# Six of nine token tiles take their u scores from a dense product; only v rows are gathered for them

## The reference

```python
# per token: 8 heads x top 16 of 128 x 128 = 16384 experts -> 128 experts
expert = take_along_axis(cand_id, top_i)
gate = softmax(top_v)
act = gelu(einsum('thkd,td->thk', u_tab[expert], xb))     # 128 dots of 1024 per token
out = einsum('thk,thkd->td', gate * act, v_tab[expert])   # 128 weighted rows of 1024
```

## Time and profile before

| | us |
|---|---|
| median of 3 runs | 4585.86 |
| lowest and highest | 4565.0, 4586.57 |
| span of the profiled execution, first to last instruction | 4574.9 |

### The profile page before, as it was taken

How to read it: one execution, slowest core, us unless ns; L and a number is a source line. 1 busy time by engine, 2 the same in 40 slices (tenths; PEclk the granted TensorE clock), 3 DMA queues, 4 the chain that set the end, 5 groups by cost and what they waited for, 6 DMA issues and landing times. The chain is left out here.

```text
span 4574.9 us, 46652 instructions
## 1 busy us (share of the span) xinstructions
PE 3277.9 (72%) x15679; PEld 1680.7 (37%) x15679; DVE 2488.2 (54%) x7735; ACT 801.6 (18%) x1284; POOL 1648.0 (36%) x1379
## 2 busy tenths in 40 slices
PE   8899997736389666686678676667666667666666
PEld 2798896636056441341145344124210101111110
DVE  2245553126764445577755454557786555555554
ACT  2232333232014113110013211211000100000000
POOL 1211104523245444442345444344333333333332
PEclk9999998968589886897789888678765666666666
DMA  7211103533789889898889898999899999999998
GB/s 278 73 58 49 39 29 131 171 118 111 274 334 407 338 354 379 345 384 341 337 348 405 345 393 356 383 375 362 354 387 360 415 404 405 409 412 409 414 411 346
DMA packets 243430, 1400.14 MB, mean 306 GB/s; under 512 B 30661, under 2 KB 47685, under 8 KB 100986
## 3 DMA queue, kind: packets, MB, share of 16 engines
q0 software_dynamic: 156672, 1140.92, 62.1%
q1 hardware_dynamic: 86522, 256.22, 15.5%
HBM read 1345.59 MB, written 51.43 MB: 305 GB/s over the span
## 5 line engine op out<-in xcount | busy, mean ns | idle before, releaser
L1057 DVE CUSTOM_DVE_ANT_0 peer_uv<-peer_uv,all_PS 128x512 f32<-128x512 f32 x2176 | 1435.3, 685 | 1164.2 <-DMA peer_uv<-in_uv,peer_idx 804.8
L996 PE MATMUL all_PS<-peer_hT,peer_sel 96*128 96x512 bf16 x2176 | 1002.4, 484 | 1027.4 <-DVE peer_halves L1057 842.5
L979 POOL DMA_INDIRECT peer_uv<-in_uv,peer_idx x1088 | 1043.4, 959 | 1756.9 <-PE all_PS L1015 1379.6
L996 PEld LDWEIGHTS all_PS<-peer_hT,peer_sel 96*128 96x128 bf16 x2176 | 203.0, 102 | 2002.9 <-DVE peer_halves L1057 1632.6
L1015 PE MATMUL all_PS<-peer_uv,peer_zw 128*32 128x512 f32 x4352 | 871.7, 849 | 2.4 <-DVE peer_zw L1077 2.4
L867 POOL TENSOR_TENSOR flow_w_lo<-flow_w,flow_w_hi 128x1024 fp32r<-128x1024 f32 (+1 forms) x204 | 460.4, 2261 | 456.5 <-ACT flow_w_hi L860 455.9
L1031 ACT ACTIVATE peer_ge<-peer_pre 128x4 f32<-128x4 f32 x272 | 55.7, 205 | 2109.7 <-DVE peer_pre L1063 2109.6
L887 PE MATMUL all_PS<-mix_h_hi,flow_w_hi 128*128 128x384 f32 (+1 forms) x672 | 279.6, 416 | 32.2 <-POOL flow_w_lo L867 31.8
L860 ACT ACTIVATE flow_w_hi<-flow_w 128x1024 fp32r<-128x1024 f32 (+1 forms) x204 | 203.5, 1003 | 359.2 <-PE all_PS L889 110.7
L888 PE MATMUL all_PS<-mix_h_lo,flow_w_hi 128*128 128x384 f32 (+1 forms) x672 | 226.3, 337 | 0.0
L889 PE MATMUL all_PS<-mix_h_hi,flow_w_lo 128*128 128x384 f32 (+1 forms) x672 | 226.1, 336 | 0.0
(11 more groups left out here) (290 smaller groups left out, 4670.4 us busy)
## 6 DMA issues: line engine op xcount, KB each, us to landing
cond_w<-in_w_ada SPq DMA_DIRECT2D x12, 2048.0 KB, 8.1
flow_w<-in_w_gate_ab SPq DMA_DIRECT2D x48, 512.0 KB, 7.1
flow_w<-in_w_query SPq DMA_DIRECT2D x48, 512.0 KB, 7.7
flow_w<-in_w_conv SPq DMA_DIRECT2D x36, 512.0 KB, 4.5
peer_uv<-in_uv,peer_idx POOLq DMA_INDIRECT x1088, 10.4
gla_w<-in_w_heads SPq DMA_DIRECT2D x24, 512.0 KB, 4.4
flow_w<-in_w_proj_b SPq DMA_DIRECT2D x24, 512.0 KB, 7.8
flow_w<-in_w_out SPq DMA_DIRECT2D x24, 512.0 KB, 8.4
```

What stands on the lines that cost most here:

```text
L979: self.nc.gpsimd.indirect_dma_start(out=self.uv[:, n % self.NUV, :], out_offset=None, in_=self.A["uv"], in_offset=bass.IndirectOffsetOnAxi ...
L996: nc.tensor.matmul(PS[:, f, :], self.sel[:, c:c + 1].broadcast_to([3 * GR, P]), self.hT[:, g % self.NH, f * 512:(f + 1) * 512], start=True ...
L1057: nc.vector.tensor_tensor_reduce(part, part, PS[:, f, :], 1.0, 0.0, ALU.mult, ALU.add, self.halves[:, d, f, e:e + 1]).then_inc(M["dotted"], 1)
```

## The change

Tiles of blocks 1 and 2 (six of nine, 768 tokens, `SCORED`) no longer gather u rows. Their pick phase also runs the whole product h @ u^T, for its block's three tiles: the transposed u table comes as 128 pieces of 0.5 MB (`u_chunks`) through the same stream, each 512 experts wide and two k-tiles deep; per piece and tile TensorE makes six matmuls of 128x512, 18 per piece, 2304 per block. A chunk of four pieces ends in three PSUM banks, which ScalarE copies and SyncE writes to a scores array in DRAM (25 MB per block). When such a token's turn comes, `fetch` issues two indirect DMAs: 128 v rows of 4 KB, and 128 single values of its scores. There is no spread, dot or join for it; gelu reads the fetched scores. The first 320 tokens go as before.

With it: slots are 18 of 4 KB per partition (a dotted token takes two, nine wide ones in all), GpSimd may fetch up to 12 tokens ahead where slots are known free, but not across the table phase; the stream's raw buffers are 4 for 2; in block 2 the low halves are made by VectorE (`make_low_on_vector`); the bf16 splits of h are made for dotted tiles alone; and each block has shares of its own. They put 148 of block 0's 296 tokens ahead of the table phase and 148 in it, and 153 of block 1's 384 ahead and 231 in it.

```diff
+SCORED = frozenset(range(3, NT))
+CHUNK, KPAIR = 512, 2
+NCHUNK, NKP = NK * NK // CHUNK, KD // KPAIR
...
-    def __init__(self, sc, sources, raws=2, pairs=4):
+    def __init__(self, sc, sources, by_vector, raws=4, pairs=4):
...
+    def make_low_on_vector(self, nc, dve, i):
+        if i < len(self.sources) and i in self.by_vector:
+            nk = self.sources[i].shape[1]
+            if i - 1 not in self.by_vector:
+                dve.wait_ge(self.low, i)
+            dve.wait_ge(self.high, i + 1)
+            nc.vector.tensor_tensor(self.lo[:, i % self.pairs, 0:nk], self.raw[:, i % self.raws, 0:nk],
+                                    self.hi[:, i % self.pairs, 0:nk].bitcast(F32), ALU.subtract).then_inc(self.low, 1)
...
-    NUV, NZ, ND, NH, AHEAD = 10, 3, 4, 6, 4
+    NUV, NZ, ND, NH, NS, AHEAD = 9, 3, 4, 6, 8, 12
...
-        for n in self.steps("pool", upto + self.AHEAD if upto else 0):
+        end = min(upto, self.limit)
+        while upto and end < min(upto + self.AHEAD, self.limit) and self.freed[end] <= max(upto - 3, 0) // BT:
+            end += 1
+        for n in self.steps("pool", end):
...
+            if self.freed[n]:
+                pool.wait_ge(self.M["v_mm"], self.freed[n])
...
+            s = self.scored_before[q]
+            if e == 0 and s >= self.NS:
+                pool.wait_ge(self.M["gelled"], q - self.NS + 1)
+            self.nc.gpsimd.indirect_dma_start(out=self.uv[:, slot, :], out_offset=None,
+                                              in_=self.A["uv"].rearrange("e (s d) -> (e s) d", s=2), in_offset=index(self.idx)
+                                              ).then_inc(self.uv_in[slot], 16)
+            self.nc.gpsimd.indirect_dma_start(out=self.score[:, s % self.NS, e:e + 1], out_offset=None,
+                                              in_=self.A[f"scores{self.part_of[u]}"].rearrange("d p (s o) -> (d p s) o", o=1), in_offset=index(self.spot)
+                                              ).then_inc(self.s_in[s % self.NS], 16)
...
+            if self.scored[n]:
+                if e == 0 and q:
+                    self.weigh(dve, q - 1)
+                continue
...
+            def chunk(j):
+                c, k2 = divmod(j, NKP)
+                u_hi, u_lo = (a[:, (w0 + j) % w.pairs].rearrange("p (k f) e -> p k (f e)", k=KPAIR) for a in (w.hi, w.lo))
+                pe.wait_ge(w.low, w0 + j + 1)
+                for i, t in enumerate(scored):
+                    m = c * nd + i
+                    tok = slice(part.at[t], part.at[t] + P)
+                    if k2 == 0 and m >= 3:
+                        pe.wait_ge(l_out, m - 2)
+                    for kk in range(KPAIR):
+                        k = KPAIR * k2 + kk
+                        nc.tensor.matmul(bank(m), h_hi[:, k, tok], u_hi[:, kk, :], start=(k == 0), stop=False)
+                        nc.tensor.matmul(bank(m), h_hi[:, k, tok], u_lo[:, kk, :], start=False, stop=False)
+                        last = nc.tensor.matmul(bank(m), h_lo[:, k, tok], u_hi[:, kk, :], start=False, stop=(k == KD - 1))
...
+                        gat.spread(pe, turns.within(j, KPAIR * i + kk + 1, KPAIR * nd))
...
             for j in range(NJ):
                 gat.gelu(act, upto(j))
+                if nd:
+                    if j % NKP == NKP - 1:
+                        emptied(j // NKP)
+                    w.make_high(nc, act, w0 + j + w.pairs)
...
-SHARES = (94, 50, 38, 42, 90, 100)
+SHARES = {0: (0, 0, 0, 0, 0, 24), 1: (45, 25, 20, 20, 40, 148), 2: (50, 25, 18, 25, 35, 231)}
```

More of the change, by code:

```diff
@@ L950, in __init__ @@
             g = rows(ORDER[u]) // GR
-            self.groups += [(u, j) for j in range(g)]
+            self.groups += [(u, j) for j in range(g) if u not in SCORED]
             self.tokens += [(u, c, j) for c in range(GR) for j in range(g)]
+        self.scored = [u in SCORED for u, c, j in self.tokens]
         self.before = [next(n for n, k in enumerate(self.tokens) if k[0] == u) for u in range(NT)] + [T]
@@ L958, in __init__ @@
         assert self.h_at == sorted(self.h_at)
+        self.rank = [0]
+        self.place, self.landed, self.freed = [], [], []
+        uses = [0] * (2 * self.NUV)
+        owner = {}
+        at = 0
+        for n, alone in enumerate(self.scored):
+            wide = 1 if alone else 2
+            slot = at % (2 * self.NUV)
+            assert slot + wide <= 2 * self.NUV
+            self.rank.append(self.rank[-1] + (not alone))
+            uses[slot] += 1
+            self.place.append(slot)
+            self.landed.append(16 * uses[slot])
+            had = [owner[slot + i] for i in range(wide) if slot + i in owner]
+            self.freed.append(max(had) // BT + 1 if had else 0)
+            for i in range(wide):
+                owner[slot + i] = n
+            at += wide
+        self.scored_before = [sum(self.scored[0:BT * q:BT]) for q in range(T // BT + 1)]
+        self.part_of = {u: part.index for part in PARTS for u in part.tiles}
         self.at = {e: 0 for e in ("pool", "pe", "act", "dve", "sp")}
-        self.loaded = 0
+        self.loaded, self.limit = 0, T
         self.ready_tiles = set()
@@ L1469, in norm_phase @@
         second = lambda i: m_rows[0:R[i], i, :]
+        ahead = lambda i: sum(d < i for d in part.dotted)
         turns = Turns(lo, hi, NJ)
@@ L1490, in _ @@
                 if stage == 2:
-                    for piece, (src, made) in enumerate(((first, one), (third, three), (fourth, four))):
-                        sp.wait_ge(made, i + 1)
+                    for piece, (src, made) in enumerate(((first, one), (third, three), (fourth, four)) if i in part.dotted else ()):
+                        sp.wait_ge(made, ahead(i) + 1)
                         sp.dma_start(A["pieces"][u, piece, 0:R[i], :], src[0:R[i], :]).then_inc(p_saved, 16)
@@ L1546, in _ @@
                     act.wait_ge(h2_done, i + 1)
[L1547 to L1550 removed]
+                    if i in part.dotted:
+                        if ahead(i):
+                            act.wait_ge(p_saved, 48 * ahead(i))
+                            act.wait_ge(two, ahead(i))
+                        nc.scalar.activation(first[0:R[i], :], x[0:R[i], i, :], ACT.Copy).then_inc(one, 1)
                     for e in range(2):
@@ L1557, in _ @@
                                              ACT.Copy).then_inc(t_out, 1)
-                    act.wait_ge(two, i + 1)
-                    nc.scalar.activation(third[0:R[i], :], second(i), ACT.Copy).then_inc(three, 1)
+                    if i in part.dotted:
+                        act.wait_ge(two, ahead(i) + 1)
+                        nc.scalar.activation(third[0:R[i], :], second(i), ACT.Copy).then_inc(three, 1)
         @block.vector
```

218 lines of the change are left out of this document (157 added, 61 removed).

## The result

| | before | after |
|---|---|---|
| median of 4 runs each, us | 4579.58 | 4859.81 |
| lowest and highest | 4565.0, 4586.57 | 4853.61, 4870.78 |
| span of the profiled execution | 4574.9 | 4857.1 |

The ratio is 1.0618, 95% interval 1.0592 to 1.0643: slower by 280 us, where the prediction had 274 (4860 for 4586).

A forecast was written before the change was run, and what follows sets the result against it. DMA bytes were taken to bound the kernel from 1251 us on, TensorE second. The terms sum to +277 us, 4852 us of span; with 11 us from span to median the forecast was 4860 us, range 4660 to 5060.

The forecast's parts named there:

- T0: Start to 1251 us (conditioning, heads, block 0): no table and the same order, so 0 us.
- T1: Block 1 ahead of its table (820 us before): 76 fewer tokens at 2.5 us each, -190 us.
- T2: Block 1's pick phase (226 us before) becomes the table phase: TensorE binds, 730 us, +504 us.
- T3: Block 2 ahead of its table (982 us before): 531 us, built from block 0, -451 us.
- T4: Block 2's table phase (261 us before): three resources within 15% of each other, 720 us, +459 us.
- T5: Last phase (1035 us before): GpSimd's two calls, 2.49 us per token, give 990 us, -45 us.
- the 11 us put on top of the span: Whole kernel: the median of the runs lies 11 us above the profiled span, so 4852 us becomes 4860.
- The rival of a cheap call: Last phase: the element call is cheap on GpSimd, the phase falls to DMA at 610 us, total 4480; chance 0.08.
- The margins over the floors of 676 and 654 us: Table phases of blocks 1 and 2: TensorE's floors times 1.08 and 1.10, giving 730 and 720 us.
- T4's third resource: DMA in block 2's table phase: 5.3 us per piece, 1.1 of it for element packets at 0.07 us each.
- The rival of dear elements: Block 2's table and last phases: 0.131 us per element packet adds 129 and 50 us, total 5040; chance 0.22.
- The rule beside T4: Element calls at 10.5 ns per packet: block 2's table phase 880 us, last phase 1113 us, time near 5140.

The follow-up runs named there:

- Run 1: The change without the fetch of the scores and gelu's wait for it; gelu reads zeros for scored tokens; 4375.39 us.
- run 2: The change with every score call made twice, the second into a buffer that nothing reads; 5708.07 us.
- Runs 3 and 4: The change with 12 table matmuls per piece for 18 (4699.79 us), then with 6, only high half by high half (4667.48 us).
- Run 7: The change with two raw buffers for four, ring as it is; 4944.47 us.
- run 8: The change with two raw buffers for four and ten wide slots for nine; 4928.89 us.
- runs 5, 6: The change with no scored tile and the shares of before: nine wide slots, four raw buffers, 4763.21 us; then ten slots, two raw buffers, 4611.85 us.

## Why the prediction was right, and where its steps were off

Each term, as predicted and as the stretches give it: T0 0, measured -13 (block 0 -23, what lies ahead +10, not explained). T1 -190, -165. T2 +504, +533. T3 -451, -457. T4 +459, +433. T5 -45, -49. Sum +277, +282. The mechanism is right, and that the time came out to the microsecond is luck: the terms miss by -13, +25, +29, -6, -26 and -4 us, which leaves +5, and the 11 us put on top of the span were 3.

- **Right for the reason given: T5.** The element call costs GpSimd what a row call costs, 1.25 us. Run 1 takes it away, run 2 doubles it, and the phase follows at 1.14 and 1.24 us per token. Run 1's figure is a lower bound, since the DMA binds there; run 2's is the price. The rival of a cheap call is excluded on the price. Its 610 us for the phase, had the call been free, was 62 too many (548 in run 1).
- **Right: the table phases are TensorE's.** 0.23 us per matmul (0.229 taken). Runs 3 and 4 confirm the bound, and show that without two thirds of the matmuls the phases stand 106 and 85 us lower. The margins over the floors of 676 and 654 us were off both ways: 759 / 676 = 1.12 for the 1.08 taken, the dear end, and 694 / 654 = 1.06 for 1.10. Run 7 points to the landing of pieces beside full rows as part of the first margin; the size of neither is otherwise shown.
- **T4's third resource was mis-sized.** "A call puts 9 packets on each engine" and 0.07 us for each: the trace has 32 packets a call, 2 per engine, and the runs give 0.12 to 0.25 us of DMA per token for my 0.63. The low end of the range that it gave, 0.12 to 1.2, was right. The rival of dear elements falls: in the last phase the DMA is at 0.71. The phase came out 26 us under its term for it.
- **T0 credited nothing to the four raw buffers.** Run 7 puts block 0 back to 536 us; they are worth 31 us here, 18 in T1 and 43 in T2, which without them would have been -147 and +576.
- **T3's 531 us is right in part by luck.** "GpSimd needs 381, inside" put the calls at nothing, but run 1 takes 42 us off the phase's 525 by taking the element calls away. What the sum did count, block 0's time and the v passes, was 48 us too dear: 531 for the 483 that run 1 leaves.
- **T1's price of 2.5 us per token was too high.** Taking 76 tokens away gave 165 us, 2.2 each, and with two raw buffers 147. The DMA share fell from 0.91 to 0.84, so the bytes alone no longer set the pace; what did is not shown. "The uv ring holds 9 wide tokens for 10: 0, with up to +20" was right for this change (4 us in this stretch and 16 in all by run 8, within the noise) and does not hold for the ring in general: where all tokens are dotted, the slot is worth 157 us (runs 5, 6).
- **The rule beside T4 did not hold.** By the Trainium skill, DMA: Bandwidth & Descriptors (Measured), about 10.5 ns per packet, I had estimated 1.5 us of DMA per element call and a last phase of 1113 us. The last phase has 986 us at a DMA share of 0.71, and runs 1 and 2 give 0.12 to 0.25 us per call; the measurement decides. The 144 packets that I put into the rule were wrong too; with the 32 of the trace it gives, as an estimate, 0.34.

The change spares DMA time and gets it: 622 us in T1 and T3. It pays with the two engines that then bind, TensorE in the table phases (+966) and GpSimd in the last phase, so that a resource that was at 0.99 falls to 0.71 with no gain.

## What to carry to other kernels

Price an indirect DMA by its calls first, then by its bytes: here a call held GpSimd for 1.25 us whether it brought 128 rows of 4 KB or 128 single values, so splitting a fetch in two halved the tokens that GpSimd could fetch in a given time. Before bytes are traded for matmuls, write down the time of each engine per stage; the gain ends at the second bound, which here stood within 15% of the first. And count ring slots in tokens in flight: one slot in ten was worth 157 us where every token took a whole one, and hardly anything (16 us, within the noise) where most took half.

## What the runs showed of the hardware

- A row call for 4 KB per partition leaves GpSimd at the same pace as one for 8 KB or for 4 B: 0.94 or 0.95 us and 0.30 us of issue, in all three.
- A call for 128 values of 4 B shows as 32 packets.
- The last phase has the same 1552 matmuls in the change and in run 1. In run 1 (first line below; L1072 is L1075 there) TensorE's weight loads waited for landings 1.2 us at a time, and the granted clock was 0.96, near the level of 2.4 GHz. In the change (second line) they waited for VectorE's weighing of a group, 8.2 us at a time, and the clock was 0.57, between the levels and nearer to 1.2 GHz. There it costs next to nothing, since GpSimd's calls alone fill 960 of the 986 us.

```profile
PEld all_PS L1072 <- DMA peer_uv<-in_uv,peer_idx: 345.3, 286, 2.6
PEld all_PS L1075 <- DVE peer_zw L1147: 792.5, 97, 13.7
```
